# Mixing the attention's probabilities unscaled and transposing them by a product with a diagonal

## The reference

```
s = einsum("bqhcd,bkhcd->bhcqk", q, k)          # c = 0, 1: two maps per head, 64 dims each
p = softmax(s, axis=-1)
w = p[:, :, 0] - lam * p[:, :, 1]               # lam: one scalar per layer
o = einsum("bhqk,bkhe->bqhe", w, v)             # 128 dims per head
```

## Time and profile before

| | us |
|---|---|
| median of 3 runs | 1305.12 (1303.79 to 1305.97) |
| the profiled execution | 1303.42 |
| its span, first to last instruction | 1301.7 |
| PE busy | 1200.7 |
| DVE busy | 751.9 |
| ACT busy | 459.6 |
| POOL busy | 133.2 |

### The profile page before, as it was taken

How to read it: one execution, slowest core, us unless ns; L and a number is a source line. 1 busy time by engine, 2 the same in 40 slices (tenths; PEclk the granted TensorE clock), 3 DMA queues, 4 the chain that set the end, 5 groups by cost and what they waited for, 6 DMA issues and landing times.

```text
span 1301.7 us, 14677 instructions
## 1 busy us (share of the span) xinstructions
PE 1200.7 (92%) x5232; PEld 946.1 (73%) x5232; DVE 751.9 (58%) x962; ACT 459.6 (35%) x687; POOL 133.2 (10%) x175
## 2 busy tenths in 40 slices
PE   0799877898999999999999999689899999999999
PEld 0588653486888888888887886337688888888887
DVE  5889988577766433345556898773543333332321
ACT  2323249834322222222224223694332222222220
POOL 6572000031000000001111000001200000000000
PEclk9899999998999999999999999899999999999999
DMA  9552131054766222255552322101222222223232
GB/s 365 188 186 102 65 95 67 1 215 157 247 224 207 85 94 98 95 207 196 194 195 79 97 81 81 49 1 49 81 86 96 95 98 95 96 96 110 100 113 81
DMA packets 39208, 158.39 MB, mean 122 GB/s; under 512 B 4528, under 2 KB 4672, under 8 KB 39040
## 3 DMA queue, kind: packets, MB, share of 16 engines
q1 hardware_dynamic: 29664, 105.02, 24.0%
q0 software_dynamic: 9504, 52.84, 10.8%
HBM read 155.75 MB, written 2.10 MB: 121 GB/s over the span
## 4 chain that ended last, share of the span: by engine, by line
PE 70%; DVE 17%; ACT 5%; POOL 3%; DMA 2%; issue 2%; DVEq 0%; ACTq 0%; SPq 0%; POOLq 0%
PE ps L1174 20%; PE ps L1175 20%; PE ps L1176 20%; DVE uc L880 4%; PE ps L1198 3%; DVE w_lo L804 3%; DVE ada_acc_early L821 2%; PE ps L1346 2%; PE ps L1202 1%; ACT prob L740 1%; DVE ada_acc_first L821 1%; DMA ada_ring_first<-ada 1%; PE ps L1213 1%; DVE neg_max L1061 1%; DMA raw<-w_stream 1%
## 5 line engine op out<-in xcount | busy, mean ns | idle before, releaser
L547 ACT ACTIVATE w_hi<-raw 128x1024 fp32r<-128x1024 f32 x196 | 207.3, 1060 | 674.3 <-PE ps L1176 537.5
L804 DVE TENSOR_TENSOR w_lo<-raw,w_hi 128x1024 fp32r<-128x1024 f32 x196 | 240.8, 1231 | 291.3 <-ACT w_hi L547 289.4
L1174 PE MATMUL ps<-h_hi,w_hi 128*128 128x512 f32 x896 | 349.8, 390 | 0.0
L1176 PE MATMUL ps<-h_lo,w_hi 128*128 128x512 f32 x896 | 349.0, 390 | 0.0
L1175 PE MATMUL ps<-h_hi,w_lo 128*128 128x512 f32 x896 | 349.0, 389 | 0.0
L1174 PEld LDWEIGHTS ps<-h_hi,w_hi 128*128 128x128 f32 x896 | 168.3, 188 | 35.1 <-DVE w_lo L804 0.4
L1176 PEld LDWEIGHTS ps<-h_lo,w_hi 128*128 128x128 f32 x896 | 168.3, 188 | 34.8
L1175 PEld LDWEIGHTS ps<-h_hi,w_lo 128*128 128x128 f32 x896 | 168.3, 188 | 34.6
L1174 PE MATMUL ps<-gu_hi,w_hi 128*128 128x512 f32 x352 | 137.4, 390 | 0.0
L1176 PE MATMUL ps<-gu_lo,w_hi 128*128 128x512 f32 x352 | 137.1, 390 | 0.0
L1175 PE MATMUL ps<-gu_hi,w_lo 128*128 128x512 f32 x352 | 137.1, 390 | 0.0
(11 more groups left out here) (172 smaller groups left out, 1260.0 us busy)
## 6 DMA issues: line engine op xcount, KB each, us to landing
raw<-w_stream SPq DMA_DIRECT2D x196, 512.0 KB, 3.3
ada_ring_late<-ada POOLq DMA_DIRECT2D x16, 768.0 KB, 8.2
ada_ring_first<-ada POOLq DMA_DIRECT2D x12, 768.0 KB, 17.0
ada_ring_gu_hi<-ada POOLq DMA_DIRECT2D x10, 768.0 KB, 5.7
ada_ring_gu_lo<-ada POOLq DMA_DIRECT2D x10, 768.0 KB, 5.1
ada_ring_early<-ada POOLq DMA_DIRECT2D x8, 768.0 KB, 10.1
ada_ring_conv<-ada POOLq DMA_DIRECT2D x4, 768.0 KB, 7.8
xT<-x_t POOLq DMA_DIRECT2D x1, 2048.0 KB, 13.8
```

What stands on the lines that cost most here:

```text
L547: act.activation(w_hi[:, u % RING, :], raw[:, u % RAW, :], ACT.Copy).then_inc(s_whi, 1)
L804: dve.tensor_tensor(w_lo[:, u % RING, :], raw[:, u % RAW, :], w_hi[:, u % RING, :].bitcast(F32), ALU.subtract).then_inc(s_wlo, 1)
L1174: pe.matmul(dst, whi, rhs[0][:, n, :], start=start, stop=False)
L1176: return pe.matmul(dst, whi, rhs[1][:, n, :], start=False, stop=stop)
```

## The change

The first map is no longer scaled. The mixing takes the raw exponentials: `row_mix` becomes -lambda times the second reciprocal times the first row sum, so that the mixed tile is the wanted one times the first row sum. The missing factor, the first reciprocal, belongs to a query, and so to a row of the untransposed tile. POOL writes a diagonal matrix with these reciprocals, `diag`, in three slots, and PE's transposes become ordinary matrix products of the mixed tile with that diagonal. DVE's wait for the scaling goes; PE gets a wait for the diagonal; POOL waits for the reciprocals and for a slot.

```diff
+        diag = sb("diag", [P, 3, P])
-        s_p0 = sem("p0_scaled")
+        s_diag = sem("diagonal_ready")
@@ gpsimd, after the loads 0 and 1 of OUT_MG[0]
+                for it in range(N_TILES):
+                    I = N_TILES * l + it
+                    pool.wait_ge(s_inv, 2 * I + 1)
+                    if it >= 3:
+                        pool.wait_ge(s_wtr, I - 2)
+                    pool.tensor_scalar(diag[:, it % 3, :], ident[:], row_inv[:, it, 0:1], 1.0, ALU.mult,
+                                       ALU.mult).then_inc(s_diag, 1)
+
+                if l == 0:
                     pool.wait_ge(s_o, HEADS)
@@ scalar
-                def scale_p0(it):
-                    I = N_TILES * l + it
-                    act.wait_ge(s_exp, 2 * I + 1)
-                    act.wait_ge(s_inv, 2 * I + 1)
-                    p0 = prob[:, it % PROBS, 0, :]
-                    act.activation(p0, p0, ACT.Copy, scale=row_inv[:, it, 0:1]).then_inc(s_p0, 1)
...
-                    if it:
-                        scale_p0(it - 1)
...
-                scale_p0(N_TILES - 1)
@@ vector
-                    dve.wait_ge(s_p0, I + 1)
                     dve.wait_ge(s_inv, 2 * I + 2)
                     dve.scalar_tensor_tensor(p0, p1, row_mix[:, it:it + 1], p0, ALU.mult, ALU.add).then_inc(s_w, 1)
...
-                    dve.tensor_scalar(row_mix[:, it:it + 1], row_inv[:, it, 1:2], neg_lam[:, l:l + 1], None,
-                                      ALU.mult).then_inc(s_inv, 1)
+                    dve.scalar_tensor_tensor(row_mix[:, it:it + 1], row_inv[:, it, 1:2], neg_lam[:, l:l + 1],
+                                             row_sum[:, it, 0:1], ALU.mult, ALU.mult).then_inc(s_inv, 1)
@@ tensor, weights_t
                     pe.wait_ge(s_w, I + 1)
+                    pe.wait_ge(s_diag, I + 1)
...
-                        mm = pe.transpose(ps[:, B_W + it % 2, kt * P:(kt + 1) * P],
-                                          prob[:, it % PROBS, 0, kt * P:(kt + 1) * P], ident[:])
+                        mm = pe.matmul(ps[:, B_W + it % 2, kt * P:(kt + 1) * P],
+                                       prob[:, it % PROBS, 0, kt * P:(kt + 1) * P], diag[:, it % 3, :],
+                                       start=True, stop=True)
```

## The result

The changed kernel takes 1309.33 us (median of 11 runs), the kernel before 1305.08 in the same comparison: 0.35% slower, ratio 1.0035 with a 95% interval from 1.0025 to 1.0044, so +4.6 us by the ratio (3.3 to 5.7; the two medians themselves lie 4.25 apart). The forecast was +6.0 and slower. The profiled execution of it has a span of 1307.6 us.

The account below looks back on a forecast made before the run. PE's dense run of matmuls was taken to bound most of the kernel; per layer -0.3 - 0.2 + 3.13 + 0.25 + 0.1 = +2.98 us, both +5.96, so 1305.12 becomes 1311.1, range 1303.5 to 1318.

Parts of the forecast that it names:

- PE is the bound from tile 6 on, ACT is not: Attended tiles: PE's starts follow without a gap, 2.50 us a tile; ACT, though full, is only as long as that.
- e = 0.45: Extra PE time, in us, of a tile's four products over its transposes, taken between the estimates 0.47 and 0.43.
- The second weight load hides: In each product on PE, a load of 0.117 us can just hide behind 128 columns; if not, e = 1.30.
- rival A: Products on PE: the second load or pass doesn't hide, e = 1.30, +21 us, 1326; chance 0.09.
- 9e less the waits = 3.13 a layer: PE in a layer's attention: 9e added, less waits of 0.52 and 0.40 us given back, makes 3.13.
- The saving in the stage, -0.5: ACT's scalings gone from a layer's attention: -0.3 us in the first tiles and -0.2 at the last mixing.
- POOL, +0.35 a layer: POOL and DVE disturbing each other: +0.25 us in tiles 2 to 5, +0.1 in tiles 12 and 14.
- Rival B: DVE's mixing waits for POOL's diagonal, about 0.9 us each instead of 0.13: +16 us, 1321; chance 0.07.
- The diagonal is in time: Tiles 5 and 6: reciprocals are ready 3.9 and 3.4 us before PE's transposes, so PE's wait costs a semaphore check.
- PE has no gap from there into the next stage, so nothing is given back later: After tiles 14 and 15, PE runs without a gap into the next stage, so the added time stays.
- The number: Whole kernel: +2.98 us a layer, +5.96 for both, giving 1311.1; chance 0.58.
- C: Products on PE: the second record costs next to nothing, e = 0, -1.4 us a layer, 1302.3; chance 0.12.
- D: Late PE waits of 0.65 and 1.20 us in a layer's attention go too: +2.3 us, 1307.4; chance 0.14.

Follow-up runs that it names:

- e1: Changed kernel with plain transposes, no ACT scaling, no POOL work and the factor left out: ratio 0.9993, -0.9 us against the kernel before.
- e4: Changed kernel with each of a tile's four products issued twice: ratio 1.0193, +25.2 us against the kernel before.
- e10: Kernel before with four y_lo of a layer moved from DVE to POOL, ACT's scaling kept: ratio 1.0005, +0.7 us against the kernel before.
- e9: e1 with four y_lo of a layer moved from DVE to POOL: ratio 0.9965, -4.6 us against the kernel before.
- e2: Kernel before with only the transposes turned into products with the identity, scaling kept: ratio 1.0039, +5.1 us against the kernel before.
- e3: Changed kernel without POOL's work, products taking the constant identity and the factor left out: ratio 1.0018, +2.3 us against the kernel before.
- e7: e1 with POOL's diagonals still written and waited for, but read by nobody: ratio 0.9998, -0.3 us against the kernel before.
- e6: The whole change in layer 1 only, layer 0 as in the kernel before: ratio 1.0025, +3.3 us against the kernel before.
- e11: e1 measured again: ratio 0.9995, -0.7 us against the kernel before.

## Why the prediction was right, point by point

- **PE is the bound from tile 6 on, ACT is not:** right. e1 took all of ACT's scaling away for 2.5 us of stage; e4 added PE work and it showed in full from tile 6 on. In the first tiles ACT sets the pace and DVE is next, as the prediction had it (e10, e9).
- **e = 0.45:** 0.50 in the run of tiles, of which the estimate from `attend` (0.47) was the nearer. The second weight load hides: 0.11 us a record (e4). The factor of 4 between transpose and product that I weighed as rival A isn't there: 0.99 against 0.49 is a factor of 2.0.
- **9e less the waits = 3.13 a layer:** right tile by tile. The same nine tiles pay e in the trace, tiles 9 and 13 are covered, and the waits give back 0.50 and 0.51 where I had 0.52 and 0.40; with e = 0.50 that is 3.5. In e2, with ACT's load as before, the stage grew by 3.74. The waits at 240.25 and 241.82 are gone there too, so they don't hang on ACT's scaling; the other 0.26 lies ahead of tile 5, whose product starts 18.66 after the first exponential instead of 18.40.
- **The saving in the stage, -0.5:** -1.0 with the products in place (e3 against e2, 56.40 against 57.38), 0.69 ahead of tile 5 (18.66 to 17.97) and 0.28 at tile 14's wait. By the experiments the stage is 3.74 - 0.98 + 0.36 = 3.12, where the prediction had 3.13 - 0.5 + 0.35 = 2.98: the product was too small by 0.6 and the saving by 0.5, and that these two cancel is luck. Ahead of tile 5 the product costs 0.26, the scaling saves 0.69 and POOL costs 0.37, together the -0.06 of the walk above, where the prediction had -0.3 + 0.25.
- **POOL, +0.35 a layer:** 0.36 (after against e3) and 0.35 (e7 against e1), but not where I put it. The mixing takes 746 ns as before, and `y_lo` 0.78 instead of 0.69, four times in a layer, 0.36. The one that is held up is POOL: its operation takes 0.98 us when the mixing starts beside it and 0.37 at the least. The Trainium skill (SBUF — State Buffer, "SBUF: two separate sides") says that a GpSimd operation and a DVE operation with two SBUF inputs lock each other out, and that whichever starts first keeps the ports for its whole instruction. The trace agrees that one of the two waits, not on which: POOL's record starts 0.07 us first (219.44 and 219.51), and the mixing isn't the longer for it. Rival B, DVE waiting about 0.9 a mixing, falls.
- **The diagonal is in time:** right; PE never waits for POOL.
- **"PE has no gap from there into the next stage, so nothing is given back later":** this step failed. It holds in layer 1: behind the last `attend` e6's execution is 0.1 us shorter than that of the kernel before, the kernel after's 0.2. Behind layer 0's attention the kernel after is 3.2 us shorter than the kernel before: 1.0 because DVE's modulation sum is ready sooner after a weight unit's transfer that lands sooner, and 2.2 up to layer 1's first exponential, most of it in the first 45 us, 12 of which had a clock of 0.86 instead of 0.59. Why the transfer lands sooner and the clock stays low for less long is open. I had read the timeline to the end of the attention, and the chain of waits only as shares.
- **The number:** in part luck. Stages of 3.14 and 3.10 less 3.2 are 3.0; low clock in a layer's first tiles, which the prediction doesn't have either, added 1.7 in the profiled execution, and the sum of 4.7 agrees with the measured 4.6 (3.3 to 5.7). The forecast of 6.0 missed both, and they partly cancel.
- **Rivals C and D:** C is wrong (e isn't near 0). D, that the late waits shrink too, is partly right: 0.65 became 0.52, which only covered tile 13, and 1.20 became 0.93, for which the forecast had 0.2.

## What to carry to other kernels

A row factor moved from one engine into another's instruction is free only if the second engine waits there: read the starts of the engine that would take it, one period long, before anything else. Here a data movement turned into arithmetic on the bound engine and cost 0.50 us a tile, to save work on an engine with time to spare. Then ask whether the factor is needed at all (a normalisation behind it removes it). And don't stop reading where the changed stage ends: compare the length of the whole stretch up to the next stage, its waits and its granted clock too, because here one layer's cost of 3.1 us was in the profiles all but met by 3 us less behind it.

## What the runs showed that I had not expected

The same POOL operation of 128x128 took 0.40 us at 206.55, with DVE idle but for the end of `row_mix`, and 0.98 beside the mixing, so POOL's mean in a profile (944 ns) says more on its neighbour than on itself. And the TensorE clock can fall to its lower level for some microseconds in the first tiles of an attention stage in one execution and not in the next of the same kernel (e1 and e11, 1.00 and 0.69 in 838:842), which moves a stage by up to 1.7 us, as much as several terms of this sum. The terms above were therefore taken from stages without a star.
